# Strassen running sums kept in PSUM, and who empties the banks

## The reference, cut to what matters

```python
h = _rmsnorm(x, norm_g[l])
proj = jnp.einsum('bsd,de->bse', h, w_in[l])
ua, va, ga, q, k, v, gb, xc, gc = jnp.split(proj, pts, axis=-1)
ya = _spatial_gating(ua, va, ...)       # mixer A
yb = _swa_sink_attention(q, k, v, ...)  # mixer B
yc = _multiscale_pool(xc, ...)          # mixer C
mix = jnp.concatenate([ya * silu(ga), yb * silu(gb), yc * silu(gc)], axis=-1)
x = x + jnp.einsum('bse,ed->bsd', mix, w_out[l])
return _rmsnorm(x, final_g)
```

## Time and profile before

| | us |
|---|---|
| median of 3 runs | 1287.9 |
| lowest and highest run | 1285.03, 1289.33 |
| span of the profiled execution | 1288.7 |
| TensorE busy in it | 1240.5 |
| VectorE busy | 862.9 |
| ScalarE busy | 521.7 |

### The profile page before, as it was taken

One profiled execution on the slowest core, in us unless ns is written; L12 is line 12 of the kernel. 1 busy time (PEld: TensorE's weight loads), 2 busy tenths in 40 slices (PEclk: granted clock), 3 DMA queues, 4 the chain that ended last, 5 costly groups with the idle time before them and its releaser, 6 DMA issues.

```text
span 1288.7 us, 16243 instructions
## 1 busy us (share of the span) xinstructions
PE 1240.5 (96%) x6182; PEld 1027.7 (80%) x6182; DVE 862.9 (67%) x1239; ACT 521.7 (40%) x947; POOL 45.5 (4%) x38
## 2 busy tenths in 40 slices
PE   7999999899998999999999999999889999999996
PEld 6778878688887888888888887787777888788885
DVE  7568677655467778878376668865668664555556
ACT  7455444435554454554343111332332422313135
POOL 3400000001310000000000000000000000000000
PEclk9999999899999999999999999999899999999999
DMA  8489336533537346455996877659988889945769
GB/s 302 125 302 323 141 141 219 189 129 116 181 131 261 131 147 233 176 197 201 351 337 239 324 281 266 229 184 354 390 312 292 296 314 380 347 153 191 288 224 354
DMA packets 98814, 314.16 MB, mean 244 GB/s; under 512 B 10128, under 2 KB 13232, under 8 KB 87344
## 3 DMA queue, kind: packets, MB, share of 16 engines
q1 hardware_dynamic: 98736, 313.12, 67.5%
HBM read 241.77 MB, written 71.30 MB: 243 GB/s over the span
## 4 chain that ended last, share of the span: by engine, by line
PE 78%; DVE 8%; DMA 6%; ACT 3%; SPq 2%; issue 2%; POOL 1%; ACTq 0%; DVEq 0%; POOLq 0%
PE n_bank L1566 15%; PE n_bank L1568 15%; PE n_bank L1567 15%; PE t_bank L1566 8%; PE t_bank L1567 8%; PE t_bank L1568 8%; PE n_bank L1760 2%; DVE w_lo L1099 2%; PE n_bank L1787 1%; DMA residual<-x_dram 1%; PE n_bank L1771 1%; PE e_bank L1566 1%; DMA raw<-w_dram 1%; PE e_bank L1568 1%; PE e_bank L1567 1%
## 5 line engine op out<-in xcount | busy, mean ns | idle before, releaser
L1099 DVE TENSOR_TENSOR w_lo<-raw,w_hi 128x1024 fp32r<-128x1024 f32 (+1 forms) x116 | 136.8, 1218 | 136.4 <-ACT w_hi L801 136.0
L1566 PE MATMUL t_bank<-op_hi,w_hi 128*128 128x512 f32 x512 | 201.9, 394 | 0.0
L1567 PE MATMUL t_bank<-op_lo,w_hi 128*128 128x512 f32 x512 | 200.5, 392 | 0.0
L1568 PE MATMUL t_bank<-op_hi,w_lo 128*128 128x512 f32 x512 | 200.1, 391 | 0.0
L1566 PE MATMUL n_bank<-w_hi,s_ring 128*128 128x512 f32 x448 | 176.9, 395 | 8.9 <-DVE t L1178 7.7
L1566 PE MATMUL n_bank<-s_ring,w_hi 128*128 128x512 f32 x448 | 179.3, 400 | 4.6 <-DVE t L1178 4.6
L1567 PE MATMUL n_bank<-w_lo,s_ring 128*128 128x512 f32 x448 | 176.1, 393 | 0.0
L1568 PE MATMUL n_bank<-w_hi,s_ring 128*128 128x512 f32 x448 | 175.9, 393 | 0.0
L1568 PE MATMUL n_bank<-s_ring,w_lo 128*128 128x512 f32 x448 | 175.4, 391 | 0.0
L1567 PE MATMUL n_bank<-s_ring,w_hi 128*128 128x512 f32 x448 | 175.3, 391 | 0.0
L801 ACT ACTIVATE w_hi<-raw 128x1024 fp32r<-128x1024 f32 (+1 forms) x116 | 113.1, 1021 | 146.7 <-PE t_bank L1568 95.4
(11 more groups left out here) (228 smaller groups left out, 1915.0 us busy)
## 6 DMA issues: line engine op xcount, KB each, us to landing
s_ring<-x_parts SPq DMA_DIRECT2D x112, 512.0 KB, 5.9
s_ring<-m_parts SPq DMA_DIRECT2D x112, 512.0 KB, 5.7
raw<-w_dram SPq DMA_DIRECT2D x46, 1024.0 KB, 4.9
y_w<-w_b_dram SPq DMA_DIRECT2D x16, 1024.0 KB, 10.7
mix<-x_t_dram SPq DMA_DIRECT2D x56, 256.0 KB, 5.5
m_parts<-stage SPq DMA_DIRECT2D x24, 512.0 KB, 7.8
x_parts<-stage SPq DMA_DIRECT2D x32, 256.0 KB, 3.0
x_parts<-mix SPq DMA_DIRECT2D x32, 256.0 KB, 3.0
```

The lines of the kernel that those rows point to most:

```text
L1099: ve.tensor_tensor(w_lo[:, J % 2, part], w_source(J)[:, part], w_hi[:, J % 2, part].bitcast(F32), ALU.subtract).then_inc(lo_done, 1)
L1566: pe.matmul(psum_out, stat[0], mov[0], start=first, stop=False)
L1567: pe.matmul(psum_out, stat[0], mov[1], start=False, stop=False)
L1568: return pe.matmul(psum_out, stat[1], mov[0], start=False, stop=last)
```

## The change

Winograd's sums P1, P1 + P6, P1 + P6 + P5 and P1 + P6 + P5 + P3 are now formed in PSUM: the products S2, S1 and S4 go on accumulating in the banks in which A11 left P1 (`fresh`, `onto`). Between two of these products the sum is read out of each bank and stays in it. A11's banks are added by VectorE to `y11` straight from PSUM. S2's are copied by ScalarE to `y21` (`copy_u`, now from PSUM), S1's by ScalarE to `y22` (`copy_v`), S4's by ScalarE to `y12` in C and A (`copy_y12`); in O and Q VectorE empties them with the residual added in the same instruction. `copy_p1` and the adds of S2 and S1 are gone. `bank_free` waits for the new emptying engine in each case.

Two residual tiles are left for `add_residual`, `y22` in step 11 and `y21` in step 13. The three loads of the buffer are issued after steps 6, 10 and 12 of O and Q in place of 6, 9 and 12; the second waits for the adds of S4, and not for `add_residual`.

```diff
@@ -605,11 +605,15 @@
...
                     sp.dma_start(y11[PAIR_O + 1][:], x_rows(0, 2)).then_inc(first_res_loaded, 16)
                 if p >= PAIR_O:
-                    i = 3 * (p - PAIR_O)
-                    for k, (at_step, m, c) in enumerate(((6, 0, 1), (9, 1, 1), (12, 1, 0))):
+                    i = 2 * (p - PAIR_O)
+                    for k, (at_step, m, c) in enumerate(((6, 0, 1), (10, 1, 1), (12, 1, 0))):
                         if j == at_step:
-                            if i + k > 0:
-                                sp.wait_ge(res_added, i + k)
+                            if k == 0 and i > 0:
+                                sp.wait_ge(res_added, i)
+                            elif k == 1:
+                                sp.wait_ge(y_added, added(p, Q_S4, ST - 1))
+                            elif k == 2:
+                                sp.wait_ge(res_added, i + 1)
                             sp.dma_start(residual[:], x_rows(m, 2 * (p - PAIR_O) + c)).then_inc(res_loaded, 16)
 
@@ -756,12 +760,12 @@
...
                 y, m, c = {Q_A11: (y11, 0, 0), Q_S4: (y12, 0, 1), Q_S3: (y22, 1, 1), Q_A22: (y21, 1, 0)}[q]
-                k = {Q_S4: 1, Q_S3: 2, Q_A22: 3}.get(q)
+                k = {Q_S3: 1, Q_A22: 2}.get(q)
                 if k is not None:
-                    sc.wait_ge(res_added, 3 * (p - PAIR_O) + k)
+                    sc.wait_ge(res_added, 2 * (p - PAIR_O) + k)
                 for st in range(ST):
                     if q == Q_S3:
-                        sc.wait_ge(y22_added, 8 * p + ST + st + 1)
+                        sc.wait_ge(y22_added, ST * p + st + 1)
                     else:
@@ -926,18 +930,6 @@
...
-            def copy_p1(p, sts):
-
-                if p == PAIR_A:
-                    sc.wait_ge(pool_in, 4)
-                elif p == PAIR_O:
-                    wait_stored(sc, "t", 5)
-                elif p == PAIR_O + 1:
-                    sc.wait_ge(a_done, 2)
-                for st in sts:
-                    wait_chain(sc, bank_done, group_done, PRODUCTS * p + Q_A11, st)
-                    sc.activation(y12[p][:, st, :], N[st][:], ACT.Copy).then_inc(p1_copied, 1)
-
@@ -950,8 +942,22 @@
...
                 for st in sts:
-                    sc.wait_ge(y_added, added(p, Q_S2, st))
-                    sc.activation(y21[p][:, st, :], y12[p][:, st, :], ACT.Copy).then_inc(u_copied, 1)
+                    wait_chain(sc, bank_done, group_done, PRODUCTS * p + Q_S2, st)
+                    sc.activation(y21[p][:, st, :], N[st][:], ACT.Copy).then_inc(u_copied, 1)
+
+            def copy_v(p, sts):
+
+                for st in sts:
+                    wait_chain(sc, bank_done, group_done, PRODUCTS * p + Q_S1, st)
+                    sc.activation(y22[p][:, st, :], N[st][:], ACT.Copy).then_inc(v_copied, 1)
+
+            def copy_y12(p, sts):
+
+                if p == PAIR_A:
+                    sc.wait_ge(pool_in, 4)
+                for st in sts:
+                    wait_chain(sc, bank_done, group_done, PRODUCTS * p + Q_S4, st)
+                    sc.activation(y12[p][:, st, :], N[st][:], ACT.Copy).then_inc(y12_copied, 1)
 
@@ -1056,10 +1062,12 @@
...
                             copy_first(pp, sts)
-                        if pp >= 0 and jj == 2 * Q_A11 + 1:
-                            copy_p1(pp, sts)
-                        if sts == (ST - 1,) and pp >= 0 and jj == 2 * Q_S2 + 1:
+                        if pp >= 0 and jj == 2 * Q_S2 + 1:
                             copy_u(pp, sts)
+                        if pp >= 0 and jj == 2 * Q_S1 + 1:
+                            copy_v(pp, sts)
+                        if pp >= 0 and jj == 2 * Q_S4 + 1 and pp < PAIR_O:
+                            copy_y12(pp, sts)
                     if was_j % 2 == 1 and was_p >= PAIR_O and was_j // 2 in (Q_A11, Q_S4, Q_S3, Q_A22):
@@ -1070,12 +1078,10 @@
...
                         job(kind, i)
-                if j == 2 * Q_S2 + 1:
-                    copy_u(p, range(ST - 1))
                 if J == step(PAIR_O + 1, 11):
...
             for st in range(ST):
-                sc.wait_ge(res_added, 6)
+                sc.wait_ge(res_added, 4)
                 sc.wait_ge(y_added, added(PAIRS - 1, Q_A22, st))
@@ -1180,49 +1186,40 @@
             def add_chain(p, q, sts):
 
                 n = PRODUCTS * p + q
+                if q in (Q_S2, Q_S1) or (p < PAIR_O and q in (Q_A12, Q_S4)):
+                    return
+                if q == Q_S4:
+                    ve.wait_ge(res_loaded, 16 * (3 * (p - PAIR_O) + 1))
+                    if p == PAIR_O:
+                        wait_stored(ve, "t", 5)
+                    else:
+                        ve.wait_ge(a_done, 2)
                 for st in sts:
-                    if q == Q_A12 and p < PAIR_O:
-                        continue
-                    if q == Q_A11:
-                        ve.wait_ge(p1_copied, ST * p + st + 1)
-                        if p < PAIR_O:
-                            ve.wait_ge(first_copied, ST * p + st + 1)
-                        else:
-                            ve.wait_ge(y_added, added(p, Q_A12, st))
-                        ve.tensor_tensor(y11[p][:, st, :], y11[p][:, st, :], y12[p][:, st, :], ALU.add
-                                         ).then_inc(y_added, 1)
-                        continue
                     wait_chain(ve, bank_done, group_done, n, st)
                     if q == Q_A12:
                         add(y11[p], st, n, (first_res_loaded, 16 * (p - PAIR_O + 1))).then_inc(y_added, 1)
-                    elif q == Q_S2:
-                        add(y12[p], st, n, (p1_copied, ST * p + st + 1)).then_inc(y_added, 1)
-                    elif q == Q_S1:
-
-                        ve.wait_ge(y_added, added(p, Q_S2, st))
-                        ve.wait_ge(u_copied, ST * p + st + 1)
-                        ve.tensor_tensor(y22[p][:, st, :], N[st][:], y12[p][:, st, :], ALU.add).then_inc(y22_added, 1)
-                        add(y12[p], st, n).then_inc(y_added, 1)
+                    elif q == Q_A11:
+                        if p < PAIR_O:
+                            add(y11[p], st, n, (first_copied, ST * p + st + 1)).then_inc(y_added, 1)
+                        else:
+                            add(y11[p], st, n, (y_added, added(p, Q_A12, st))).then_inc(y_added, 1)
                     elif q == Q_S4:
-                        add(y12[p], st, n, (y_added, added(p, Q_S1, st))).then_inc(y_added, 1)
+                        ve.tensor_tensor(y12[p][:, st, :], N[st][:], residual[:, st, :], ALU.add).then_inc(y_added, 1)
                     elif q == Q_S3:
-                        add(y22[p], st, n, (y22_added, 8 * p + st + 1)).then_inc(y22_added, 1)
+                        add(y22[p], st, n, (v_copied, ST * p + st + 1)).then_inc(y22_added, 1)
                         add(y21[p], st, n, (u_copied, ST * p + st + 1)).then_inc(y_added, 1)
                     else:
                         add(y21[p], st, n, (y_added, added(p, Q_S3, st))).then_inc(y_added, 1)
 
             def add_residual(p, k):
 
-                i = 3 * (p - PAIR_O) + k
-                ve.wait_ge(res_loaded, 16 * (i + 1))
+                i = 2 * (p - PAIR_O) + k
+                ve.wait_ge(res_loaded, 16 * (3 * (p - PAIR_O) + k + 2))
                 if k == 0:
-                    ve.wait_ge(u_copied, ST * (p + 1))
-                    ve.wait_ge(y_added, added(p, Q_S1, ST - 1))
-                elif k == 1:
-                    ve.wait_ge(y22_added, 8 * p + ST)
+                    ve.wait_ge(v_copied, ST * (p + 1))
                 else:
                     ve.wait_ge(y_added, added(p, Q_S3, ST - 1))
-                y = (y12, y22, y21)[k][p]
+                y = (y22, y21)[k][p]
                 ve.tensor_tensor(y[:], y[:], residual[:], ALU.add).then_inc(res_added, 1)
                 ve.wait_ge(res_added, i + 1)
 
@@ -1244,9 +1241,9 @@
...
                 if half == 0:
-                    ve.wait_ge(y_added, added(PAIR_C, Q_S4, ST - 1))
+                    ve.wait_ge(y12_copied, ST * (PAIR_C + 1))
                 else:
-                    ve.wait_ge(y22_added, 8 * PAIR_C + 8)
+                    ve.wait_ge(y22_added, ST * (PAIR_C + 1))
                 src, rstd = (t12, rstd_0) if half == 0 else (t22, rstd_row)
@@ -1517,7 +1514,7 @@
...
                 if J == step(PAIR_A, 10):
-                    ve.wait_ge(y_added, added(PAIR_A, Q_S4, ST - 1))
+                    ve.wait_ge(y12_copied, ST * (PAIR_A + 1))
                     scale_rows(4, t12, rstd_0[:])
@@ -1540,7 +1537,7 @@
...
                         job(kind, i)
-                for k, t in enumerate((8, 11, 13)):
+                for k, t in enumerate((11, 13)):
                     if p >= PAIR_O and j == t:
@@ -1561,11 +1558,11 @@
...
 
-            def three(psum_out, stat, mov, first, last):
-
-                pe.matmul(psum_out, stat[0], mov[0], start=first, stop=False)
```

(29 more changed lines are left out.)

## The result

| | before | after |
|---|---|---|
| median of 9 runs each, us | 1287.2 | 1294.8 |
| ratio | | 1.0054, 95% interval 1.0040 to 1.0067 |
| span of the profiled execution | 1288.7 | 1294.5 |
| VectorE busy | 862.9 | 824.5 |
| ScalarE busy | 521.7 | 526.7 |

The change takes 58 instructions and 38 us from VectorE and makes the kernel 0.54% slower: 7.0 us by the ratio, 7.6 by the two medians. The forecast was 1293.5 in a range of 1287 to 1298.5, and a span of 1294.3.

A forecast was written before the change was run, and what follows sets the result against it. TensorE was taken to bound the Strassen part, so only late-released banks count, not VectorE's saved time. Gains 1.1 + 6.5 = 7.6 and losses 0.3 + 1.6 + 4.2 + 7.1 = 13.2 gave median 1293.5, slower by 5.6; range 1287 to 1298.5.

The forecast's parts named there:

- The adds that leave VectorE: 56 adds, 38 us of VectorE, worth only TensorE's waits at A8 (gain 1.1) and A10 (gain 6.5).
- A11's banks on VectorE: At A3 and A4, VectorE instead of ScalarE releases A11's banks: loss 0.3 us, bounds 0 and 1.1.
- Ring slots in A12: Step A12's ring slots, queued behind a weight load, land late for the earlier TensorE: loss 1.6 us, bounds 0 and 3.
- The residual of step 11: In O11 and Q11 VectorE waits for the later-issued tile: loss 4.2 us in O (1.8 to 6.1), 7.1 in Q (4.8 to 8.7).
- the slack: At the end of Q, the last add began 1.2 us behind the matmuls; half assumed used up, taking 0.6 off the loss.
- the correction from span to median: The profiled span of 1288.7 us was taken as 0.8 above the median of the runs; 0.8 was subtracted at the end.
- The clock term: TensorE's clock falls after a wait: 1.7 us added in O and in Q, 2.7 gained back at A10.
- transfers eat the gain at A10: Rival, chance 0.13: the DMA queue is full at A10, ring slots come as late as before, the 6.5 is lost; 1298.4 us.
- The load is quicker: Rival, chance 0.08: the residual lands 7.2 us after issue, not 9.1; O loses 0.6, Q 5.2; 1288.0 us.
- the wait at O0 shrank: Rival, chance 0.10: the waits at O0 and O2 shrink as pair A's stores find more time, some 3 us; 1290.5 us.
- The clock did not stay full: Rival denied here, chance 0.07: the clock stays full behind the new waits, so 2 x 1.7 is not paid; 1290.1 us.
- VectorE did wait: Rival denied here, chance 0.12: the step 11 residual lands when VectorE is free, no wait in O11 or Q11; 1282.2 us.

The follow-up runs named there:

- e3: The kernel after, but in pairs C and A VectorE and not ScalarE copies S4's banks, where its adds for S4 stood; 1301.2 us, ratio 1.0118.
- f1: The kernel after with the second residual load after step 9, plus A12's ring slots issued ahead of two weight loads in A10; 1282.2 us, ratio 0.9967.
- e1: The repaired kernel: the kernel after with the second residual load issued after step 9 and not step 10; 1283.25 us, ratio 0.9970.
- e2: The kernel before with its second residual load issued after step 10 in place of step 9, nothing else; 1299.0 us, ratio 1.0094.
- e4: The kernel after, its load still late, but VectorE adds that residual behind S3's adds (and `finish_first` in Q11); 1285.4 us, ratio 0.9992.
- The two edits against them: Each alone on the repaired kernel: third residual load after step 11, not 12 (1281.4 us); final norm's weights loaded in O3, not A12 (1278.7 us).
- f4: The repaired kernel with ring slots first in A10, third residual load after step 11 and final norm's weights in O3; 1275.2 us, ratio 0.9911.

## Why the prediction was right, point by point

The sum was 1.3 us short of the median after. Each loss lies within its bounds, and the two gains, for which none were given, came out as forecast. That the total is so close is in part luck, as said below.

- **The adds that leave VectorE** are worth two waits and not their 38 us. A8 and A10 gave 1.2 and 6.5. e3 shows that A10's comes from the other list: without S2's and S1's adds, but with S4 still behind VectorE's jobs, the wait is 4.51. At A8 no run separates the adds that went from the new place of the copy.
- **A11's banks on VectorE** cost 0.4 in A3 and A4 for the 0.3 of the timeline. No run took this apart.
- **Ring slots in A12**: 2.2 for 1.6. The load ahead of them took 14.6 us for 13.5, and so all four came later. f1 shows that the order in the queue moves these waits, but not that it saves anything.
- **The residual of step 11** is the step that decided. e1 takes it away, e2 makes it in the kernel before, e4 moves the wait behind the adds. In O the load landed after 10.0 us and not 9.1, so TensorE started 3.4 late for 2.5. In Q it was quicker (8.3): the low part of Q13 came 5.2 later, counted from the start of Q11, and not 6.0, while the clock took 1.6 and the slack gave back 0.6, and the end moved by 6.2 for 7.1. The two errors nearly cancel, which is luck. The forecast took the median of six loads for both places; in the kernel before the second load took 10.0 in O and 9.1 in Q, and over the ten profiles it took 9.3 to 10.1 in O and 7.7 to 9.1 in Q.
- **What was off**: the correction from span to median. The profiled execution after took 1296.28 for a span of 1294.5, so 1.8 lie around the span, and if it was as much before, that profiled execution took 1290.5. This is 2.6 over the median of its three runs, and not 0.8, and 3.3 over the 1287.2 of the nine. The profiled execution after lies only 1.5 over its median, so the medians are 7.6 apart and the spans 5.8. The forecast started from 1287.9, 0.7 too high, and this hid a part of the 2.0 by which its change of 5.6 was short. Executions differ by more than that: the kernel after ran from 1289.95 to 1299.85.
- **The clock term** was right in size (1.5 in O12 and 1.6 from Q13 on, for 1.7) but is no constant, as the last section shows.
- Of the rivals, "transfers eat the gain at A10" was true for 2.2 of 6.5. "The load is quicker" came halfway in Q (8.3), not in O, and the wait at O0 shrank by 0.25 alone. The clock did not stay full, and VectorE did wait.

## What to carry to other kernels

When a buffer gets one more reader, all loads that reuse it move, and the load's place in the program is part of the price of the change. Look at what stands behind the wait in the list of that engine: here waits of 6.9 and 5.2 us for 1 MB held the adds that free PSUM banks, and in the last pair the operands of the next step. Taking work from an engine pays only where a wait ends in that work; count the waits and their place before the microseconds. And once one such wait is found, look for its twins: the waits at Q0 and O0 stand in the kernel before as well. The two edits against them gave 1.8 and 4.5 us by the medians, more than the 3.0 by which the repaired change beats the kernel before; they were tried on the repaired kernel alone.

## What the runs showed of the hardware

The same idle of TensorE is followed by a lower clock in one execution and not in the next. At O2 the wait for VectorE is 2.25 us in both of these; the kernel after, then e1 (timeline of TensorE, then the stretch with its granted clock, third from the end):

```profile
985.92 0.50 PE L1563 MATMUL n_bank<-w_hi,s_ring 128*128 128x512 f32 x1 [2.25 <-DVE t L1184]
```
```profile
986.00:997.00 11.00, 11.00 (x49) 9.10 (x50) 10.90 (x11) 0.76 (x2) 0.00 (x0) 1.00 1.01 347
```
```profile
983.54 0.50 PE L1563 MATMUL n_bank<-w_hi,s_ring 128*128 128x512 f32 x1 [2.25 <-DVE t L1184]
```
```profile
984.00:996.00 12.00, 12.00 (x48) 9.71 (x47) 11.32 (x12) 1.14 (x2) 0.00 (x0) 0.86 0.90 307
```

The step takes 11.0 us in the one and 12.6 in the other. The idle at O2 is the same in all ten profiles of this study, and the step was the long one in four. Nor is it the longer idle that loses the clock: at Q0 an idle of 2.10 was followed by a step of 12.6 us in the kernel after, and an idle of 2.44 by one of 11.0 in e1. What decides between the two, no run here shows. Such a wait costs itself and, in some executions, 1.6 us more at O2 and up to 2.8 at O0 (step 13.67 for a clean 10.88, behind an idle of 3.34 in the kernel after; 11.0 behind one of 2.37 in f4). A fixed clock term is therefore an average.

The Trainium skill's page TensorE: Matmul & The Clock Gate, section Loop structure matters more than you think, holds that a copy out of PSUM by VectorE leaves the clock up, in a loop where the next matmuls follow immediately. Here they did not follow immediately: at O12 TensorE idled 3.24 us for an add out of PSUM, and the granted clock of the 12 us behind it was 0.87. At Q13 the idle was for the low part, and the clock was 0.86.
